# A new order for the opening of a two-layer encoder kernel: norm vector first, w in halves among x, keys and values as first unit

## The reference

```python
h = rmsnorm(x, norm_g[l])                      # x / sqrt(mean(x^2) + 1e-6) * g
proj = h @ w_in[l]                             # 1024 x 7936
# columns: a_q 512, a_k 128, a_v 128, a_gate 512, b_u, b_v, b_gate 512 each,
#          c_q, c_f, c_i, c_gate 512 each, merge 3 * 1024
out_a = sliding_window_attention(rope(a_q), rope(a_k), a_v, sinks) * silu(a_gate)
out_b = spatial_gating(gelu(b_u), gelu(b_v), ...) * silu(b_gate)
out_c = rmsnorm(hgrn2(c_q, 1 - f, c_i, log f)) * silu(c_gate)   # f from c_f and bounds
y = sum_n(sigmoid(merge_n + b_merge_n) * (out_n @ w_branch[l, n])) @ w_out[l]
x = x + y
```

## Time and profile before

| | us |
|---|---|
| median of 3 runs | 1046.14 |
| profiled execution, own time | 1045.28 |
| its span | 1043.4 |
| TensorE busy | 1018.4 |
| first projection matmul | 20.38 |
| job 2 begins | 40.3 |
| first scores begin | 76.25 |

### The profile page before, as it was taken

The page is one execution under the profiler, slowest core; times in us unless marked ns, Lnnn a source line. Parts: engine busy times, 40 slices in busy tenths (PEclk is TensorE's granted clock), DMA queues, the critical chain, the costliest instruction groups (busy, mean ns, idle before and its releaser), DMA issues.

```text
span 1043.4 us, 15327 instructions
## 1 busy us (share of the span) xinstructions
PE 1018.4 (98%) x6389; PEld 857.8 (82%) x6389; DVE 650.5 (62%) x832; ACT 521.0 (50%) x809; POOL 302.8 (29%) x156
## 2 busy tenths in 40 slices
PE   5899999999999999999999999999999999999997
PEld 4689899888888888888887889988888888888876
DVE  6876894799635444355548579578984353544552
ACT  5667665676453323232448666577556333332333
POOL 3321111532422313143212110163243232323420
PEclk9899999999999999999999999999999999999999
DMA  6242222222223232333234222122231232323502
GB/s 196 71 129 74 81 83 82 60 62 82 82 61 120 82 101 82 100 101 122 84 114 136 81 83 59 64 82 81 82 101 57 85 102 81 101 81 101 191 12 80
DMA packets 95412, 94.71 MB, mean 91 GB/s; under 512 B 2272, under 2 KB 93616, under 8 KB 95344
## 3 DMA queue, kind: packets, MB, share of 16 engines
q1 hardware_dynamic: 95136, 93.44, 28.9%
q0 software_dynamic: 80, 0.26, 0.2%
q10 hardware_dynamic: 128, 0.04, 0.0%
HBM read 91.64 MB, written 2.10 MB: 90 GB/s over the span
## 4 chain that ended last, share of the span: by engine, by line
PE 95%; DVE 2%; issue 1%; ACT 1%; DMA 1%; POOL 0%; DVEq 0%; POOLq 0%; ACTq 0%
PE pj L480 28%; PE pj L482 27%; PE pj L481 27%; PE mx L607 2%; PE mx L480 1%; PE mx L482 1%; PE mx L481 1%; DVE sum_sq L1196 1%; PE mx L570 1%; PE mx L667 1%; PE mx L547 1%; PE mx L635 1%; PE mx L555 1%; PE mx L645 1%; DMA pos_int<-in_positions 1%
## 5 line engine op out<-in xcount | busy, mean ns | idle before, releaser
L1066 POOL TENSOR_TENSOR w_lo<-w_raw,w_hi 128x512 fp32r<-128x512 f32 (+1 forms) x92 | 198.5, 2158 | 564.5 <-ACT w_hi L783 564.3
L480 PE MATMUL pj<-h_hi,w_hi 128*128 128x512 f32 x832 | 330.7, 397 | 1.5 <-issue 1.5
L482 PE MATMUL pj<-h_hi,w_lo 128*128 128x512 f32 x832 | 325.1, 391 | 0.0
L481 PE MATMUL pj<-h_lo,w_hi 128*128 128x512 f32 x832 | 325.0, 391 | 0.0
L783 ACT ACTIVATE w_hi<-w_raw 128x1024 fp32r<-128x1024 f32 (+1 forms) x184 | 160.6, 922 | 164.3 <-PE pj L482 162.4
L1187 DVE TENSOR_TENSOR w_lo<-w_raw,w_hi 128x512 fp32r<-128x512 f32 (+1 forms) x92 | 159.8, 1737 | 64.9 <-ACT w_hi L783 64.7
L480 PEld LDWEIGHTS pj<-h_hi,w_hi 128*128 128x128 f32 x832 | 156.9, 189 | 36.5 <-issue 4.6
L482 PEld LDWEIGHTS pj<-h_hi,w_lo 128*128 128x128 f32 x832 | 156.7, 188 | 33.3
L481 PEld LDWEIGHTS pj<-h_lo,w_hi 128*128 128x128 f32 x832 | 157.0, 189 | 32.3 <-issue 1.0
L1253 DVE TENSOR_TENSOR merge_gate<-pj,rstd 128x512 f32<-128x512 f32 x48 | 33.2, 691 | 162.9 <-PE pj L482 162.9
L863 ACT ACTIVATE merge_gate<-merge_gate,small 128x512 f32<-128x512 f32 x48 | 34.3, 715 | 89.3 <-DVE merge_gate L1253 89.3
(11 more groups left out here) (240 smaller groups left out, 1526.2 us busy)
## 6 DMA issues: line engine op xcount, KB each, us to landing
w_raw<-in_w_in SPq DMA_DIRECT2D x60, 1024.0 KB, 5.5
w_raw<-in_w_branch SPq DMA_DIRECT2D x24, 512.0 KB, 3.4
w_raw<-in_w_out SPq DMA_DIRECT2D x6, 1024.0 KB, 5.1
x_tokens<-in_x SPq DMA_DIRECT2D x4, 512.0 KB, 9.0
w_raw<-in_w_in SPq DMA_DIRECT2D x4, 512.0 KB, 4.0
w_raw_last<-in_w_out SPq DMA_DIRECT2D x2, 1024.0 KB, 7.3
sp_w_rows<-in_sp_w SPq DMA_DIRECT2D x2, 512.0 KB, 4.7
out<-out_low SPq DMA_DIRECT2D x4, 256.0 KB, 2.0
```

Source lines behind the costliest of these rows:

```text
L480: pe.matmul(bank, wh, ah, start=first, stop=False)
L481: pe.matmul(bank, wh, al, start=False, stop=False)
L482: return pe.matmul(bank, wl, ah, start=False, stop=final)
L1066: return pool.tensor_tensor(out=dst, in0=full, in1=hi.bitcast(f32), op=ALU.subtract)
```

## The change

Units and jobs: keys and values become one unit of 256 columns, `("kv", 0)`, and the first; the four query jobs follow as jobs 2 to 5. Job 0 is keys, job 1 values. From job 6 on the order is as before, 94 jobs for each layer, 47 units instead of 48. The ropes start with the keys; `swap_keys` waits for the first rope only. `LATE` is gone. In layer 1 the jobs are in the new order too, and the sums of squares are made as before.

Opening: norm_g has its own tile, transfer and transpose, and is transposed first. Unit 0 of w comes in two halves of 512 KB, between the pieces of x. Positions are loaded by SyncE behind x. TensorE transposes four parts of x, starts on jobs 0 and 1 and transposes the other four inside them. ScalarE and VectorE make high and low parts of h from the PSUM banks, and the copies into `XT` come later. VectorE does the low parts of both halves of unit 0. GpSimd makes no squares: VectorE takes mean and variance of each token from `x_tokens` (`bn_stats`, `bn_aggr`), mean^2 + variance goes through logarithm and exponential into `RT`, a diagonal matrix of it (`DG`) is multiplied by ones in four matmuls of 128 columns after job 3, and ScalarE copies the result into `RS`. The sines, the bounds and their VectorE steps are moved behind the first evacuations. The loads of the attention's and the spatial mixing's side data follow unit 4 instead of unit 3.

The diff, cut to its core:

```diff
...
-UNITS = ([("q", 0), ("q", 1), ("k", 0), ("v", 0)]
+UNITS = ([("kv", 0), ("q", 0), ("q", 1)]
...
-JOBS = [(u, t) for u in range(NU) for t in range(1 if UNITS[u][0] in ("k", "v") else 2)]
...
+JOBS = [(u, t) for u in range(NU) for t in range(2)]
...
-LATE = {0: 2, 1: 2, 3: 4, 4: 5}
-ROPE_AT = (2, 3, 3, 4, 5)
+ROPE_AT = (2, 3, 4, 5, 6)
+ROPE_FIRST = (3, 4, 4, 5, 6)
...
-            if kind in ("k", "v"):
-                return (buf[:, :, 0:P], w(AK if kind == "k" else AV, P))
+            if kind == "kv":
+                return (buf, w(AK, 2 * P))
...
-            sp.dma_start(CST[:, :], consts[:, :]).then_inc(cst_in, 16)
-            for j in range(KT // 2):
...
+            def load_x(j):
...
-                if j == 1:
-                    load_weights(sp, 0)
+            buf, src = unit_load(0)
+            sp.dma_start(CST[:, :], consts[:, :]).then_inc(cst_in, 16)
+            load_x(0)
+            sp.dma_start(buf[:, 0:4, :], src[:, 0:4, :]).then_inc(first_half, 16)
+            load_x(1)
+            sp.dma_start(buf[:, 4:8, :], src[:, 4:8, :]).then_inc(raw_in[0], 16)
+            load_x(2)
+            load_x(3)
+            sp.dma_start(POSI[:, :], positions[0].partition_broadcast(P)).then_inc(pos_in, 16)
             for v in range(1, RB):
...
-                if v == RB:
+                if v == RB + 1:
...
                     pe.wait_ge(xT_evac, k - 5)
+                    pe.wait_ge(xg_lo, k - 5)
                 for tb in range(TB):
                     last = pe.transpose(x_bank(k)[:, tb * P:(tb + 1) * P], XTOK[:, tb, k * P:(k + 1) * P], ID)
                 last.then_inc(xT_done, 1)
-                if k == 1:
-                    pe.wait_ge(vec_in, 16 * 4)
-                    pe.transpose(M[0][:, 0:80], VR[0:80, :], CST[0:80, 0:80]).then_inc(vecT_done, 1)
-            pe.wait_ge(fill_done, 1)
+            pe.wait_ge(cst_in, 16)
+            pe.wait_ge(norm_in, 16)
+            pe.transpose(M[1][:, 0:16], VN[0:16, :], CST[0:16, 0:16]).then_inc(normT_done, 1)
+            for k in range(4):
+                transpose_x(k)
+            pe.wait_ge(vec_in, 16 * 3)
+            pe.transpose(PJ[2][:, 0:64], VR[0:64, :], CST[0:64, 0:64]).then_inc(vecT_done, 1)
+            pe.wait_ge(p_norm, 1)
...
-                        pe.wait_ge(w_lo_vec, layer * NU + u + 1)
+                        if layer * NU + u > 0:
+                            pe.wait_ge(w_lo_vec, layer * NU + u + 1)
...
+                        if n == 0 and layer == 0:
+                            if k in (2, 3):
+                                if k == 2:
+                                    pe.wait_ge(p_vec, 1)
+                                transpose_x(2 * k)
+                                transpose_x(2 * k + 1)
+                            if k == KT // 2:
+                                pe.wait_ge(w_lo_vec, 1)
...
-                    if n == 0:
-                        if layer == 0:
-                            pe.wait_ge(xT_evac, KT)
-                        pe.wait_ge(ss_ready, layer + 1)
+                    if n == 1 and layer == 0:
+                        pe.wait_ge(xT_evac, KT)
+                    if n == 3 and layer == 0:
+                        pe.wait_ge(fill_done, 1)
+                        pe.wait_ge(p_diag, 1)
+                        for tb in range(TB):
+                            last = pe.matmul(M[4][:, tb * P:(tb + 1) * P], ONE[:, :], DG[:, tb, :],
+                                             start=True, stop=True)
+                        last.then_inc(norm_sum, 1)
+                    if n == 0 and layer > 0:
...
-            act.dma_start(VR[0:16, :], norm_g.rearrange("l (k p) -> (l k) p", p=P)).then_inc(vec_in, 16)
...
+            act.dma_start(VN[:, :], norm_g.rearrange("l (k p) -> (l k) p", p=P)).then_inc(norm_in, 16)
...
+            def first_h(k):
                 act.wait_ge(xT_done, k + 1)
+                act.activation(HH[:, k, :], x_bank(k)[:, :], ACT.Copy, scale=VL[:, 0, k:k + 1]).then_inc(xg_hi, 1)
+            def x_evac(k):
+                act.wait_ge(xg_lo, k + 1)
                 act.activation(XT[:, k, :], x_bank(k)[:, :], ACT.Copy).then_inc(xT_evac, 1)
-                act.wait_ge(xT_evac, k + 1)
-                scaled_hi(k, 0).then_inc(xg_hi, 1)
+            act.wait_ge(fill_done, 1)
+            act.activation(RO[:, 0:1], EP, ACT.Copy)
+            act.wait_ge(p_norm, 1)
+            first_h(0)
+            first_h(1)
+            act.wait_ge(first_half, 16)
+            split_half(0, 0)
+            first_h(2)
+            first_h(3)
+            x_evac(0)
+            x_evac(1)
+            weights_in(act, 0)
+            split_half(0, 1)
+            x_evac(2)
+            x_evac(3)
+            first_h(4)
+            first_h(5)
+            first_h(6)
+            first_h(7)
+            x_evac(4)
+            x_evac(5)
             split_hi(1)
-            act.wait_ge(fill_done, 1)
-            act.wait_ge(p_half, 1)
-            act.activation(SH[:, :], ANG[:, :], ACT.Sin)
-            act.activation(CH[:, :], TRN[:, :], ACT.Sin, bias=PIH, scale=-1.0).then_inc(p_sin, 1)
-            act.wait_ge(p_diff, 1)
-            act.activation(LBT[:, 12:20], LBT[:, 4:12], ACT.Exp).then_inc(p_exp, 1)
+            x_evac(6)
+            x_evac(7)
...
+                def first_rstd():
+                    act.wait_ge(p_ms, 1)
+                    chained(act.activation(RT, MS, ACT.Ln, bias=EP, scale=1.0))
+                    act.activation(RT, RT, ACT.Exp, scale=-0.5).then_inc(p_rstd, 1)
...
+                    act.wait_ge(p_half, 1)
+                    act.activation(SH[:, :], ANG[:, :], ACT.Sin)
+                    act.activation(CH[:, :], TRN[:, :], ACT.Sin, bias=PIH, scale=-1.0).then_inc(p_sin, 1)
+                def bounds_exp():
+                    act.wait_ge(p_diff, 1)
+                    act.activation(LBT[:, 12:20], LBT[:, 4:12], ACT.Exp).then_inc(p_exp, 1)
+                def rstd_row():
+                    act.wait_ge(norm_sum, upto(norm_sum, 1))
+                    act.activation(RS[:, :], M[4][:, :], ACT.Copy).then_inc(rstd_ready, 1)
...
-                phase[1].append((token_rstd,))
-                phase[ROPE_AT[4] + 2].append((swap_keys,))
-                phase[FIRST[("v", 0)] + 3].append((values,))
+                if layer == 0:
+                    phase[0].append((first_sines,))
+                    phase[2].append((first_rstd,))
+                    phase[2].append((bounds_exp,))
+                    phase[3].append((rstd_row,))
+                else:
+                    phase[1].append((token_rstd,))
+                phase[ROPE_AT[4]].append((swap_keys,))
+                phase[V_JOB + 3].append((values,))
...
-                    for late, when in LATE.items():
-                        if when == n:
-                            evac(late)
                     for f, *a in phase[n]:
                         f(*a)
-                    if n < NJ and n not in LATE:
+                    if n < NJ:
                         evac(n)
...
-            pool.dma_start(POSI[:, :], positions[0].partition_broadcast(P)).then_inc(pos_in, 16)
...
-            split_lo(0)
-            for k in range(KT):
-                pool.wait_ge(xT_evac, k + 1)
-                if k >= 2:
-                    pool.wait_ge(p_ss, k - 1)
-                pool.tensor_tensor(out=TP[:, k % 2, :], in0=XT[:, k, :], in1=XT[:, k, :], op=ALU.mult)\
-                    .then_inc(p_sq, 1)
...
-            dve.wait_ge(pos_in, 16)
-            dve.wait_ge(cst_in, 16)
-            pchain(dve.tensor_copy(ANG[:, :], POSI[:, :]))
...
+            def angle_first():
+                dve.wait_ge(pos_in, 16)
+                pchain(dve.tensor_copy(ANG[:, :], POSI[:, :]))
...
+            def first_low(k):
+                dve.wait_ge(xg_hi, k + 1)
+                dve.scalar_tensor_tensor(out=HL[:, k, :], in0=x_bank(k)[:, :], scalar=VL[:, 0, k:k + 1],
+                                         in1=HH[:, k, :].bitcast(f32), op0=ALU.mult, op1=ALU.subtract)\
+                   .then_inc(xg_lo, 1)
...
+                dve.wait_ge(w_hi, 2 * v + 1 + half)
+                dve.tensor_tensor(out=lo_part(v, half), in0=raw_part(v, half), in1=hi_part(v, half).bitcast(f32),
+                                  op=ALU.subtract).then_inc(w_lo_vec if half else w_lo, 1)
...
+            dve.wait_ge(normT_done, 1)
+            dve.tensor_copy(VL[:, :, 0:8], M[1][:, 0:16].rearrange("p (l c) -> p l c", l=2)).then_inc(p_norm, 1)
+            dve.wait_ge(p_norm, 1)
+            dve.wait_ge(cst_in, 16)
+            first_low(0)
+            first_low(1)
+            split_half(0, 0)
+            first_low(2)
+            first_low(3)
...
+            for c, cn, r0 in ((8, 24, 0), (32, 4, 48)):
...
+            dve.tensor_copy(LBT[:, 24:32], PJ[2][:, 56:64]).then_inc(p_vec, 1)
+            split_half(0, 1)
+            first_low(4)
+            first_low(5)
+            angle_first()
+            first_low(6)
```

(93 more changed lines are left out.)

114 lines of the change are left out of this document (50 added, 64 removed).

## The result

The changed kernel takes 1037.95 us (median of six executions, 1035.17 to 1040.68), the kernel before 1046.14 (1045.22 to 1046.74) on the same chip: a ratio of 0.9922 (0.9904 to 0.994). The forecast was 1037.8. But no execution took about 1037.8: three took 1035.2 to 1035.5 and three 1040.4 to 1040.7.

What follows compares the result with a forecast made beforehand. TensorE was taken as the bound, busy 1018.4 of 1043.4 us. Matmuls start 9.4 us earlier, but a moved wait (4.8) and slow clock (2.4) leave 8.3 gained by the scores; off median 1046.14, 1037.8 us, range 1034.0 to 1041.5.

Runs made afterwards that it cites:

- run 2: Changed kernel, with ScalarE's high parts of unit 5 held in the first layer until the last rope is done: 1036.71 us, ratio 0.9905.
- run 10: Changed kernel, with all eight transposes of x ahead of the first unit and the ten bounds steps behind the last rope: 1031.64 us, ratio 0.9861.
- run 4: Changed kernel, with all eight transposes of x ahead of the first unit instead of four inside it: 1036.10 us, ratio 0.9906.
- run 3: Changed kernel, with the ten small bounds steps moved from before the last rope to behind it in the first layer: 1034.99 us, ratio 0.9894.
- run 8: Changed kernel, with many edits joined that reorder the first layer's chain to the scores, bounds last: 1028.47 us, ratio 0.9832.
- run 6: Changed kernel, with positions issued first from GpSimd's queue, as in the kernel before: 1042.43 us, ratio 0.9948.

## What to carry to other kernels

When a wait is moved, sum the engine that ends last at the *new* place with every operation that a faster TensorE will set going at that moment; a margin under one operation's length is no margin if another engine can hold that one operation. When executions of one kernel fall into two levels, look for a single instruction with two durations and for who started first, and then for where the clock falls: with that instruction freed, two levels 3.4 us apart remained (run 2). The repair may be to move idle small work (here ten steps of 0.2 us) behind the instruction others wait for. And a stop is paid twice where it takes the clock: run 10 against run 4 took 3.8 us of wait for the last rope away and gained 4.5.

## What the runs showed of the hardware

- VectorE instructions that began while GpSimd made a low part ended only behind it: 0.69 became 2.72 (`q_rot`), 0.68 became 2.89 (`rope_sin`), and even a step on 128x8 elements that takes 0.17 took 2.26.
- The granted clock of one kernel fell at different points of the same stop of 5.6 us (38.3 in one execution, 40.6 in another, 41.3 in run 3), stayed at 0.50 for 3.4 to 6.8 us, and also fell in a stop of only 2.6 us (run 2). Stops of 0.7 to 1.5 us (runs 3 and 10) did not take it. From the first matmul of the first unit the slow spacing lasted 3.7 us in one execution of the changed kernel and 2.7 in another, 1.2 in run 4 and 1.4 in run 8. Run 4 has more transposes ahead of it and run 8 has not, so these runs do not show that the transposes shorten it. The Trainium skill (TensorE: Matmul & The Clock Gate, "The HAM clock gate") says that the number of slow matmuls varies for one kernel; by that rule, these traces agree.
- A broadcast of 256 KB, issued first and from GpSimd's queue, delayed the second part of x by 2.3 us, three times what its bytes would take (run 6).
